# One core, one encoder step: carried weight tiles at the early stages, another window softmax, and an inverse that keeps one factor in the other half of the partitions

## What is computed

```python
def mem_kv(mem, g, w_mem_kv):
    k, v = jnp.split(rmsnorm(mem, g) @ w_mem_kv, 2, axis=-1)
...
# window attention, chunks of 64 queries over the own chunk and the one before
    s = jnp.einsum('bnqkgd,bnskd->bnkgqs', qc, kb).astype(jnp.float32) * (hd ** -0.5)
...
    p = sink_softmax(s, sink.reshape(SWA_KV, G)[None, None, :, :, None, None])
    o = jnp.einsum('bnkgqs,bnskd->bnqkgd', p.astype(v.dtype), vb)
...
# the delta rule, step by step
        Sa = jnp.einsum('bhvk,bhk->bhv', S, a_t)
        S = S * w_t[:, :, None, :] + Sa[..., None] * b_t[:, :, None, :] + v_t[..., None] * k_t[:, :, None, :]
```

## Time and profile before

| | us |
|---|---|
| median of 3 runs | 2768.72 (2767.32 to 2776.0) |
| the profiled execution | 2771.12 |
| its span | 2769.3 |
| in-projection / prepare / windows / delta (from stage starts in the trace) | 335.9 / 188.0 / 168.1 / 599.0 |
| mixing, cross attention, feed-forward | 1478.3 |

### The profile page before, as it was taken

How to read it: one execution, slowest core, us unless ns; L and a number is a source line. 1 busy time by engine, 2 the same in 40 slices (tenths; PEclk the granted TensorE clock), 3 DMA queues, 4 the chain that set the end, 5 groups by cost and what they waited for, 6 DMA issues and landing times. The chain is left out here.

```text
span 2769.3 us, 48761 instructions
## 1 busy us (share of the span) xinstructions
PE 2556.8 (92%) x20214; PEld 2399.9 (87%) x20214; DVE 1554.0 (56%) x2419; ACT 964.6 (35%) x1498; POOL 307.1 (11%) x587
## 2 busy tenths in 40 slices
PE   8999798686999999995899996899999999999997
PEld 7999766475899999993899995789999899999997
DVE  5665356667344544444665422558854788368863
ACT  5332056322123222222313301345433544345542
POOL 0111123300000000000001200011111211123320
PEclk9999899798999999997999998999999999999999
DMA  4222345554322223222765326643344433443343
GB/s 152 65 65 82 121 171 208 170 155 128 119 82 88 75 88 115 70 79 76 241 204 180 109 87 219 191 153 130 125 139 153 140 126 125 147 164 130 127 126 97
DMA packets 225100, 361.43 MB, mean 131 GB/s; under 512 B 46368, under 2 KB 163488, under 8 KB 224096
## 3 DMA queue, kind: packets, MB, share of 16 engines
q1 hardware_dynamic: 212496, 333.92, 37.7%
q0 software_dynamic: 6144, 21.24, 2.1%
q10 hardware_dynamic: 6240, 3.15, 0.4%
HBM read 275.77 MB, written 83.38 MB: 130 GB/s over the span
## 5 line engine op out<-in xcount | busy, mean ns | idle before, releaser
L2065 PE MATMUL ffn_bank<-ffn_shared_x_hi,ffn_shared_w_hi 128*128 128x384 f32 x1248 | 421.5, 338 | 16.5 <-DVE ffn_shared_w_lo L2055 7.1
L2065 PE MATMUL ffn_bank<-ffn_shared_x_lo,ffn_shared_w_hi 128*128 128x384 f32 x1248 | 419.0, 336 | 0.0
L2065 PE MATMUL ffn_bank<-ffn_shared_x_hi,ffn_shared_w_lo 128*128 128x384 f32 x1248 | 418.8, 336 | 0.0
L2048 ACT CAST ffn_shared_w_hi<-ffn_shared_w_raw 128x1024 fp32r<-128x1024 f32 (+1 forms) x228 | 234.6, 1030 | 428.3 <-PE ffn_bank L2065 385.5
L2065 PE MATMUL mix_bank<-mix_operand,mix_w_hi 128*128 128x384 f32 x1344 | 346.5, 337 | 30.8 <-DVE mix_operand L2245 29.8
L2055 DVE TENSOR_TENSOR ffn_shared_w_lo<-ffn_shared_w_raw,ffn_shared_w_hi 128x1024 fp32r<-128x1024 f32 (+1 forms) x228 | 272.8, 1197 | 173.9 <-ACT ffn_shared_w_hi L2048 173.9
L2065 PEld LDWEIGHTS mix_bank<-mix_operand,mix_w_hi 128*128 128x128 f32 x1344 | 244.3, 189 | 34.6 <-DVE mix_w_lo L2055 22.6
L2065 PEld LDWEIGHTS ffn_bank<-ffn_shared_x_hi,ffn_shared_w_hi 128*128 128x128 f32 x1248 | 236.1, 189 | 19.5 <-issue 13.5
L2065 PEld LDWEIGHTS ffn_bank<-ffn_shared_x_hi,ffn_shared_w_lo 128*128 128x128 f32 x1248 | 235.9, 189 | 0.8 <-issue 0.3
L2065 PEld LDWEIGHTS ffn_bank<-ffn_shared_x_lo,ffn_shared_w_hi 128*128 128x128 f32 x1248 | 235.7, 189 | 0.0
L2065 PE MATMUL mix_bank<-mix_operand,mix_w_lo 128*128 128x384 f32 x672 | 225.4, 335 | 0.0
(11 more groups left out here) (366 smaller groups left out, 4768.2 us busy)
## 6 DMA issues: line engine op xcount, KB each, us to landing
ffn_shared_w_raw<-in_w_up SPq DMA_DIRECT2D x132, 512.0 KB, 3.4
win_win_raw<-in_w_in SPq DMA_DIRECT2D x52, 512.0 KB, 4.0
ffn_shared_w_raw<-in_w_down SPq DMA_DIRECT2D x48, 512.0 KB, 3.5
scratch_gates<-delta_gates SPq DMA_DIRECT2D x72, 192.0 KB, 4.2
mix_pieces<-scratch_gates SPq DMA_DIRECT2D x72, 192.0 KB, 3.2
ffn_shared_w_raw<-in_w_xo SPq DMA_DIRECT2D x24, 512.0 KB, 3.5
scratch_features<-prepare_a_r_b_k POOLq DMA_DIRECT2D x12, 768.0 KB, 4.3
ffn_shared_w_raw<-in_w_down SPq DMA_DIRECT2D x24, 384.0 KB, 3.1
```

What stands on the lines that cost most here:

```text
L2048: act.copy(self.hi[j % self.splits][:, 0:kt], self.raw[j % self.raws][:, 0:kt]).then_inc(self.rounded, 1)
L2065: mm = pe.matmul(bank, w[s][:, k, :], x, start=(start and k == 0 and i == 0), stop=(stop and k == kt - 1 and i == 2), skip_group_check=True)
```

## The change

Three edits.

1. `Units` gets two raw tiles; the load of tile j+2 follows the split of tile j.
2. `CARRY = 4`: the first four halves (two units) of prepare's dense product run on PE after the last of the in-projection, into two PSUM banks (`carried`) that live across the stages, and likewise two memory units of windows after prepare. Prepare grows from 42 to 51 slots, six of the 16 memory tiles move into it, and windows shrinks from 53 to 42 slots with chunks two slots apart. Rounding, squares and root of the memory tokens move into the in-projection, 28 slots ahead of its end; SP loads them there when the convolution and recurrence stores have landed. The softmax of a chunk is rewritten: DVE reduces the maxima straight from PSUM, ACT takes four exponentials from PSUM with scale, bias and an accumulated sum, and DVE only normalises, one slot later. `score` of chunk c waits for the exponentials and for the copy of v of chunk c-1.
3. In delta the gram is formed twice (`gram_both_ways`), in either half of the partitions; K is kept in the half opposite to T. `off_times_t` puts its output in the opposite half, and `merge` writes its two products alternately; it has one semaphore, and waits for both copies of Z.

```diff
 class Units:
-        self.raw = st.sb(f"{tag}_raw", [P, KD, P])
+        self.raw = [st.sb(f"{tag}_raw{s}", [P, KD, P]) for s in range(2)]
...
-        self.load_at = {s: j + 1 for s, j in self.lo_at.items() if j + 1 < len(tiles)}
+        self.load_at = {s: j + 2 for s, j in self.lo_at.items() if j + 2 < len(tiles)}
...
     def load(self, eng, j):
-        if j:
-            eng.wait_ge(self.rest, j)
-        eng.dma_start(self.raw[:], self.tiles[j][0]).then_inc(self.arrived, 16)
+        if j >= 2:
+            eng.wait_ge(self.rest, j - 1)
+        eng.dma_start(self.raw[j % 2][:], self.tiles[j][0]).then_inc(self.arrived[j % 2], 16)
...
     def score(self, pe, c):
         if c:
-            pe.wait_ge(S("probs"), c)
+            pe.wait_ge(S("exp"), 4 * c)
+            pe.wait_ge(S("v_turned"), c)
...
     def exponentials(self, act, c):
+        for n, (g, b) in enumerate(self.UNITS):
+            act.activation(x[:, n, 0:nk], self.scored(c, b)[:, g], ACT.Exp, scale=HD ** -0.5, bias=z[:, 1, n:n + 1],
+                           accum_out=z[:, 2, n:n + 1]).then_inc(S("exp"), 1)
+        act.wait_ge(S("sink_centred"), c + 1)
+        act.activation(z[:, 4], z[:, 3], ACT.Exp).then_inc(S("exp_sink"), 1)
...
+    def maxima(self, dve, c):
         for b in range(2):
+            dve.tensor_reduce(z[:, 0, b::2], self.scored(c, b), AX.X, ALU.max).then_inc(S("maxed_part"), 1)
+        dve.wait_ge(S("maxed_part"), 2 * c + 2)
+        dve.scalar_tensor_tensor(out=z[:, 1], in0=z[:, 0], scalar=-HD ** -0.5, in1=self.nsink[:], op0=ALU.mult, op1=ALU.min).then_inc(S("maxed"), 1)
...
+    def normalise(self, dve, c):
+        dve.tensor_tensor(z[:, 5], z[:, 2], z[:, 4], ALU.add).then_inc(S("norm_of_row"), 1)
+        dve.reciprocal(z[:, 0], z[:, 5]).then_inc(S("norm_of_row"), 1)
+        dve.tensor_tensor(x[:, :, 0:nk], x[:, :, 0:nk], z[:, 0].rearrange("p (n o) -> p n o", o=1).broadcast_to([P, 4, nk]),
                           ALU.mult).then_inc(S("probs"), 1)
...
 def stage_in_projection(nc, env, io):
+                    if slot == MEM_AT - 3:
+                        sp.wait_ge(S("conv_stored"), 32 * KM)
+                        sp.wait_ge(S("recurrence_stored"), 16 * KM)
+                        sp.wait_ge(S("conv"), 2 * KM)
+                        sp.dma_start(mem, io["memt"]).then_inc(S("mem_in"), 16)
...
-                for slot in range(END + 4):
+                for slot in range(END + CARRY):
                     if slot < END:
                         dense.half(pe, slot, operands, banks, x_ready)
+                    else:
+                        dense.half(pe, slot, operands, env["carried"])
+                    if slot == MEM_AT + 5:
+                        mem_sums()
...
 def stage_prepare(nc, env, io):
-        LORA_AT = {x: START + x for x in range(AHEAD)}
-        BODY_AT = {x: START + 4 + 3 * x for x in range(UNITS)}
-        LORA_AT |= {x + AHEAD: BODY_AT[x] for x in range(UNITS - AHEAD)}
+        LORA_AT = {x: START + CARRY + 2 + x for x in range(AHEAD)}
+        BODY_AT = {x: START + CARRY + 6 + 3 * x for x in range(UNITS)}
+        LORA_AT |= {x + AHEAD: BODY_AT[x] - 1 for x in range(UNITS - AHEAD)}
...
 def stage_windows(nc, env, io):
-        WINDOW_AT = {c: START + 3 + 3 * c for c in range(NCH)}
-        SCORE_AT = {h: START + 22 + h for h in range(NH)}
+        WINDOW_AT = {c: START + 4 + 2 * c for c in range(NCH)}
+        SCORE_AT = {h: START + 14 + 2 * h for h in range(NH)}
...
 def stage_delta(nc, env, io):
-                        tt(M[s][:, KT], L[s], squares("off2", 1, [KM])[:, 0], ALU.mult).then_inc(S("T_off"), 1)
+                        tt(M[s][:, KT], Lopp[s], squares("off2", 1, [KM])[:, 0], ALU.mult).then_inc(S("T_off"), 1)
...
+                def gram_both_ways(t, left, right):
+                    for p, c in cells:
+                        for s in range(2):
+                            mm_(INV[rows(c), s, col(p)], left(s, p, chunk(c)), right(s, p, chunk(c)), start=True, stop=True)
+                            mm = mm_(INV[rows(1 - c), s, col(KM + p)], left(s, p, chunk(c)), right(s, p, chunk(c)), start=True, stop=True)
...
                 def off_times_t(t, i):
+                    pe.wait_ge(S("T"), inverted(t) + 2 * i + 2)
                     for s in range(2):
-                        pe.wait_ge(S("T"), inverted(t) + 2 * i + s + 1)
-                            mm = mm_(INV[rows(c), s, col(p)], O_[s][rows(c), i, p, :], M[s][rows(c), KTT(t % 2), p, :], start=True, stop=True)
+                            mm = mm_(INV[rows(1 - c), s, col(p)], O_[s][rows(c), i, p, :], M[s][rows(c), KTT(t % 2), p, :], start=True, stop=True)
...
                 def merge(t, i):
+                    pe.wait_ge(S("Z_copied"), 2 * (merges[t] + i) + 2)
                     for s in range(2):
-                        pe.wait_ge(S("Z_copied"), 2 * (merges[t] + i) + s + 1)
                         for p, c in cells:
+                            z, kt = Zm[s][rows(1 - c), p, :], M[s][rows(1 - c), KT, p, :]
                             if i < len(levels(t)) - 1:
-                                mm_(INV[rows(c), s, col(p)], Zm[s][rows(c), p, :], M[s][rows(c), KT, p, :], start=True, stop=True)
-                        for p, c in cells:
-                            mm = mm_(INV[rows(c), s, col(KM + p)], M[s][rows(c), KT, p, :], Zm[s][rows(c), p, :], start=True, stop=True)
-                        mm.then_inc(S("merged"), 1)
+                                mm_(INV[rows(1 - c), 0, col(s * KM + p)], z, kt, start=True, stop=True)
+                            mm = mm_(INV[rows(c), 1, col(s * KM + p)], kt, z, start=True, stop=True)
+                    mm.then_inc(S("merged"), 1)
...
 -    slots["prepare"] = (begin, begin + 42)
-    begin += 42
+    early, held = 6, CARRY // 2
+    slots["prepare"] = (begin, begin + 51)
+    after = begin + 51
     for i in range(2 * KD):
-        tiles.append((io["w_mem_kv"][i], "mem", [(0, NMEM, (begin + 4 + 3 * i, begin + 5 + 3 * i))]))
+        if i < early:
+            part = (begin + 36 + 2 * i, begin + 37 + 2 * i)
+        elif i < early + held:
+            part = (after + 2 * (i - early), after + 2 * (i - early) + 1)
+        else:
+            part = (after + CARRY + 4 * (i - early - held), after + CARRY + 4 * (i - early - held) + 2)
```

296 lines of the change are left out of this document (168 added, 128 removed).

## The result

The changed kernel takes 2711.14 us in the median (2708.21 to 2714.71), the kernel before 2772.36 us on the same occasion: a ratio of 0.978, with a 95% interval of 0.9764 to 0.9795. The forecast was 2693 within 2662 to 2726, and faster. So the sign and the range held, and the gain was smaller than forecast: 61 us between the two profiled executions (2771.12 and 2709.99), not 76.

A forecast was written before the change was run, and what follows sets the result against it. PE was taken as nearly full in delta but idle 83 us in prepare and windows; +4.9 + 4.3 - 60 - 25 = -75.8 from 2771.1 gives 2695.3, or 2693 by the median, range 2662 to 2726.

The forecast's parts named there:

- In-projection, forecast +4.9: In-projection stage: 4.4 us for the memory tokens' 16 sum matmuls plus 0.5 for carried halves nearly hidden behind the last stores.
- Prepare, forecast +4.3: Prepare stage in three parts: +2.7 to the first turn of v, -11 between bodies 0 and 9, +12.6 after body 9.
- To the first turn of v: Start of prepare: four carried halves saved, six still ahead of body 0, first split waits for ACT's inputs; +2.7, bounds -3 to +7.
- from body 0 to 9: Middle of prepare: gate and norms earlier, turns of k and b later, covering chunk beginnings; -11 us, bounds -13 and 0.
- from body 9 to the end: Tail of prepare: six memory tiles and two carried, 22.7 us, about 10 filling PE's wait; +12.6, bounds +5 and +25.
- Windows, forecast -60: Windows stage: memory prologue gone, shorter softmax chain, 12.0 us a pair of chunks; 168.1 to 108 us, bounds 94 and 128.
- the two limits: Windows, per pair of chunks: SP's queue, with a weight load waiting for a split, 11.2 us; PE's own work, 11.6.
- the third rival: Prepare's tail +9 and exponentials at 0.8 us each, a pair of chunks 13.6 us, +10: time 2712; chance 0.19.
- Delta, forecast -25: Delta: alternating four array quarters saves 0.85 us in each of 34 merges, -29; the second gram costs +4.6.
- That the four quarters don't overlap in this order: Rival in delta: successive matmuls reading the same partition half don't overlap, merge stays at 29 ns, delta +4.6, time 2722; chance 0.12.
- That SP's queue does not hold the windows: Rival in windows: chunk loads come early enough, PE alone is the bound, 94 us instead of 108, time 2679; chance 0.15.
- The slow rival: Windows: SP's queue becomes a chain through all engines, a pair takes 23.7 us, windows 186, time 2771 or more; chance 0.02.

## Why the prediction was right, and where it was not

**In-projection, forecast +4.9, measured +6.0.** Right, as far as it can be told: in the other runs that start from the changed kernel the stage took 340.5 to 343.7 us. The sums took 3.6 instead of 4.4 us. The carried halves were hidden as forecast: without them (the run that doesn't carry) the in-projection is no shorter, 342.9 us. What the forecast left out is that their gain is small too: 8.5 us of work taken out of prepare brought 4 to 6.

**Prepare, forecast +4.3, measured +11.3.** To the first turn of v +1.8 (forecast +2.7), from body 0 to 9 -15.5 (forecast -11, bound -13), and from body 9 to the end +25.1 (forecast +12.6, bounds +5 and +25). The middle part went beyond its bound because the step of an undisturbed body was misread. The prediction took 12.4 us, but two of the steps before were 11.6 already; one of them ends at 405.55 and begins here:

```profile
393.98 0.55 PE L1058 MATMUL prepare_work<-masks,prepare_r_k_v 128*128 128x128 f32 x3
```

Nine bodies at 11.6 are 104.4, so 20 us could be won and not 13. In the changed kernel seven of the nine steps are 11.6, and two chunk beginnings still take 13.2 and 14.9.

The term that was mis-sized is the last: it counted 22.7 us of PE work and let 10 of them fill the wait at the end. That the splits queue on DVE was named, but as a reason against the low end and without a price. The price is a circle from PE over ScalarE and VectorE back to PE, 3 to 6 us for five of the tiles. That it runs over the place of the split was shown by the run with the split first for the memory tiles: 13 to 16 us less in prepare, and a tail of 45.6 us, near the 47.0 (34.4 + 12.6) that the forecast counted without a circle. The run with the exponentials first showed that opening one of its two ways alone is not enough. The prediction had named as a sign of being wrong a tail of prepare longer than 59 us, and it is 59.5, 62.1 in the second execution: by its own sign it was wrong here, though the whole time lay within the range.

**Windows, forecast -60, measured -47.7.** From the score of chunk 2 to that of chunk 15 were 79.3 us, forecast 78. So the sum over the chunks was right, and partly by luck: a pair in the middle takes 11.1 us and not 12.0, and waits for a chunk's loads made up most of the rest. Of the two limits that the prediction held for nearly equal, the run with the chunk loads first showed that PE sets the pace in the middle, and that SP's queue held the chunks up only at the first chunks and from the sample's softmax on. The mis-sized terms are the two ends. Score 2 was forecast at +18 and came at +24.8. Score 0 stands behind a dense half in its slot, and that waited 6.95 us for a split; score 2 waited for its loads behind the sample's and the weight tile's. The two faster versions, which change the order at the beginning and the loads together, brought score 2 to +19.8 and +22.0. From the last score to the end were 16.3 us instead of 12; no run tested why. The four exponentials cost less than taken, 1.39 instead of 1.7 us (below); the row of 0.42 that the prediction used had 256 elements in each partition, and these have 128. So the 0.8 for each that the third rival counted on is not there.

**Delta, forecast -25, measured -30.1.** Right in mechanism, the size 5 us off and just beyond the bound of -29. A merge lost 0.92 us, not 0.85; taken to the next dense half each, all 34 are 31.3 us shorter together. The second gram costs 0.46 us in eight tiles, as taken, and 1.15 in the first, 4.8 in all. Not forecast was that eight of the products O·T, those with a part of the solve behind them, take 0.18 us less each, 1.4 in all. These make -27.9; the other 2.2 us lie mostly at the two ends of the stage, and their cause stays open. DVE's sums did not become a wait: PE's list of waits in delta names none for them, as the thin cover of half a microsecond allowed.

**The rivals.** That the four quarters don't overlap in this order (0.12) is wrong: successive instructions that read the same half of the partitions start within 0.01 us of each other, and the merge ran at 15 ns an instruction. The rule that the prediction took from the Trainium skill, "TensorE: Matmul & The Clock Gate", "Part 3: Packing small matmuls — row/col tiling", that weight loads overlap running matmuls only where the row group differs, did not hold here: the second weight load shown starts at 765.97, 0.01 us behind the first, and runs while the first matmul does (765.97, 0.27 us long), though both read the same half. The measurement decides. That SP's queue does not hold the windows (0.15) is right for the middle and wrong in its time: even with the chunk loads first the stage took 118.8 us and not 94, with 22.8 ahead of score 2 and 21.0 behind score 15. The longer tail of prepare (0.19), 2712, is the nearest to the result, and that is half luck. Its +9 for the tail was the right cause, with 12.5 measured; its +10 for the exponentials was not there, and the ends of windows and delta's larger gain took its place by chance. The slow rival's 186 us for windows should be 184 (108 and 76); nothing hangs on it.

**The sum.** The four stages missed by +1.1, +7.0, +12.3 and -5.1 us. That the whole came within the range owes something to delta and to the bodies of prepare, whose gains were forecast too small.

**Two raw tiles.** The prediction gave them no term. The run with one raw tile says 8 to 11 us, so a part of the measured gain belongs there, and it was set against the other terms unseen.

## What to carry to other kernels

When a piece of work is moved into another stage, its busy time can be only half of its price: 12.6 of 25.1 us in the tail of prepare here. Write down for each engine what stands ahead of it and behind it in that stage, and look for a circle: an engine that waits for something that stands, on another engine, behind what waits for the first. Opening one way of the circle here brought nothing while a second was left; moving the piece that both ways share, the split, brought 13 to 16 us.

The small matmuls here, which use a quarter of the array each, gained 0.51 us a merge from operands placed so that the two products lie in different quarters, and another 0.41 from an order in which the products take turns. Forecast both ends of a stage apart from its middle: here the time from chunk 2 to chunk 15 was right to 2%, and the misses were ahead of chunk 2 and behind the last.

## What the runs showed of the hardware that was not expected

An exponential with an accumulated sum is two instructions in the trace (start, duration, engine, line):

```profile
603.18 0.37 ACT L278 ACTIVATE windows_scores<-windows_score_bank,windows_stat 128x128 f32<-128x128 f32 x1 [2.74 <-DVE windows_stat L324]
603.45 0.19 ACT L278 ACTIVATION_READ_ACCUMULATOR windows_scores<-windows_score_bank,windows_stat 128x1 f32 x1
603.54 0.36 ACT L278 ACTIVATE windows_scores<-windows_score_bank,windows_stat 128x128 f32<-128x128 f32 x1
...
604.57 0.21 ACT L281 ACTIVATE windows_stat<-windows_stat 128x4 f32<-128x4 f32 x1
```

The next exponential starts 0.36 us after the first, before the reading of its sum has ended in the trace, so in this row of four the reading adds little. The next instruction after the four starts at 604.57, 1.39 us after the first. That is 0.35 for each, less than the 0.42 that the prediction had taken as the least from a row of twice the size.

In the run with the merge in blocks, the instructions did not start block by block: the next block uses the other two quarters of the array, and its first instructions start after ten of the first block. 64 instructions in blocks of 16 take 1.50 us to the next work there, between the 1.09 of full alternation and the 2.01 of blocks that all use the same two quarters.
